# Offsetting the second recurrent stream of a two-block transformer kernel by 24 steps, with the modulation's products spread over every third step and lambda's vectors loaded at the start

## The reference, cut to what matters

```
def step(state, inp):                        # rwkv7, 8 heads of 64, 512 positions
    r_t, w_t, k_t, v_t, kk_t, b_t = inp
    sa = einsum('bhij,bhj->bhi', state, -kk_t)
    state = state * w_t[:, :, None, :] + sa[..., None] * b_t[:, :, None, :] \
          + v_t[..., None] * k_t[:, :, None, :]
    return state, einsum('bhij,bhj->bhi', state, r_t)
...
lam_full = exp(sum(lam[0] * lam[1])) - exp(sum(lam[2] * lam[3])) + lambda_init   # differential attention
bias = rel_bias[_t5_bucket(dist)]                                                # a table by distance
...
mod = (silu(c) @ ada_w[l] + ada_b[l]).reshape(B, 3, 3, 1, D)                     # second block, layer l
```

## Time and profile before

| what | value |
|---|---|
| median of three executions | 4032.23 us (4018.51 to 4037.8) |
| profiled execution, its own time | 4021.96 us |
| its span | 4020.2 us |
| mean granted TensorE clock | 0.946 of full speed |
| PE busy | 3671.3 us (91%) |
| DVE busy | 1983.7 us (49%) |
| ACT busy | 1333.8 us (33%) |
| POOL busy | 106.4 us (3%) |
| the recurrent loop | 57.5 to 492.0 us of the span |

### The profile page before, as it was taken

How to read it: one execution, slowest core, us unless ns; L and a number is a source line. 1 busy time by engine, 2 the same in 40 slices (tenths; PEclk the granted TensorE clock), 3 DMA queues, 4 the chain that set the end, 5 groups by cost and what they waited for, 6 DMA issues and landing times.

```text
span 4020.2 us, 46185 instructions
## 1 busy us (share of the span) xinstructions
PE 3671.3 (91%) x19278; PEld 2833.2 (70%) x19278; DVE 1983.7 (49%) x3434; ACT 1333.8 (33%) x2347; POOL 106.4 (3%) x204
## 2 busy tenths in 40 slices
PE   6687668699899989999899989999999889999998
PEld 4575545478688868886766768887888756677886
DVE  4767635555564655455454453334333455444333
ACT  3223213453353532232433332223222344433222
POOL 0000010000000000000000000000000000000000
PEclk9798878799999999999999999999999989999999
DMA  4232241025333325453211223332333211032332
GB/s 148 80 100 75 70 136 34 22 84 158 100 125 100 118 79 198 127 176 102 75 32 43 62 75 100 94 95 84 94 95 99 91 54 39 27 92 85 95 95 68
DMA packets 100672, 364.30 MB, mean 91 GB/s; under 512 B 11664, under 2 KB 11728, under 8 KB 99952
## 3 DMA queue, kind: packets, MB, share of 16 engines
q1 hardware_dynamic: 75888, 272.14, 21.9%
q0 software_dynamic: 24576, 89.21, 7.0%
HBM read 359.20 MB, written 2.10 MB: 90 GB/s over the span
## 4 chain that ended last, share of the span: by engine, by line
PE 87%; DVE 9%; ACT 3%; DMA 1%; issue 1%; POOL 0%; DVEq 0%; ACTq 0%; POOLq 0%
PE ps_run L369 86%; PE ps_run L613 1%; DVE rt L1548 1%; DVE nrm L1555 1%; DVE nrm L1558 1%; DVE mb L1635 1%; DVE HL L1555 1%; DVE rt L1558 1%; DMA mb<-ada 0%; ACT nrm L939 0%; ACT bias L939 0%; ACT L939 0%; ACT rt L939 0%; DVE rt L1552 0%; DVE rt L1555 0%
## 5 line engine op out<-in xcount | busy, mean ns | idle before, releaser
L369 PE MATMUL ps_run<-HH,wh 128*128 128x512 f32 x2800 | 1128.9, 403 | 91.0 <-DVE HL L1555 48.1
L369 PE MATMUL ps_run<-HL,wh 128*128 128x512 f32 x2800 | 1104.8, 395 | 0.0
L369 PE MATMUL ps_run<-HH,wl 128*128 128x512 f32 x2800 | 1103.6, 394 | 0.0
L1548 DVE TENSOR_TENSOR wl<-st,wh 128x1024 fp32r<-128x1024 f32 x511 | 625.6, 1225 | 875.6 <-ACT wh L939 874.8
L939 ACT ACTIVATE wh<-st 128x1024 fp32r<-128x1024 f32 x511 | 537.8, 1053 | 752.3 <-PE ps_run L369 751.8
L369 PEld LDWEIGHTS ps_run<-HH,wh 128*128 128x128 f32 x2800 | 533.0, 190 | 247.8 <-DVE HL L1555 70.2
L369 PEld LDWEIGHTS ps_run<-HH,wl 128*128 128x128 f32 x2800 | 534.0, 191 | 114.0
L369 PEld LDWEIGHTS ps_run<-HL,wh 128*128 128x128 f32 x2800 | 534.6, 191 | 108.2 <-issue 3.8
L369 PE MATMUL ps_run<-AH,wh 128*128 128x512 f32 x1040 | 413.2, 397 | 0.0
L369 PE MATMUL ps_run<-AL,wh 128*128 128x512 f32 x1040 | 409.9, 394 | 0.0
L369 PE MATMUL ps_run<-AH,wl 128*128 128x512 f32 x1040 | 409.8, 394 | 0.0
(11 more groups left out here) (333 smaller groups left out, 3743.9 us busy)
## 6 DMA issues: line engine op xcount, KB each, us to landing
st<-wst SPq DMA_DIRECT2D x511, 512.0 KB, 3.5
mb<-ada POOLq DMA_DIRECT2D x144, 512.0 KB, 3.9
cw<-cw POOLq DMA_DIRECT2D x4, 1024.0 KB, 6.2
X<-xT SPq DMA_DIRECT2D x8, 256.0 KB, 7.9
X<-xT POOLq DMA_DIRECT2D x8, 256.0 KB, 4.2
out<-X SPq DMA_DIRECT2D x8, 256.0 KB, 2.0
mb<-cond POOLq DMA_DIRECT2D x2, 512.0 KB, 6.9
cs<-rope POOLq DMA_DIRECT2D x2, 512.0 KB, 3.8
```

What stands on the lines that cost most here:

```text
L369: i = self.e.matmul(out, lhsT, rhs, start=start, stop=stop, skip_group_check=True)
L1548: self.e.tensor_tensor(out, a, b, op).then_inc(*self.w.done(*points))
```

## The change

Three edits. Stream 1 does nothing in its first 24 turns, and so runs 24 steps behind stream 0 on each engine. Products of the modulation are made in steps with n % 3 equal to 2. `lt` and `lam` get a place of their own, and POOL loads `lt` right after the constants. The loop is then 340 + 24 = 364 single steps long: 24 of stream 0 with an empty turn between them (n from 0 to 47), 146 pair-steps (n from 48 to 339), and 24 of stream 1 alone (n from 340 to 363).

```
+def later(steps, gen):
+    for _ in range(steps):
+        yield
+    yield from gen
...
+        self.lt, self.lam = self.sb("lt", 4), self.sb("lam", 4)
...
-        self.lt, self.lam = r("lt", 4), r("lam", 4)
...
# in Pe.program, Act.program and Dve.program
-        for n, _ in enumerate(alternate(self.rwkv(0), self.rwkv(1))):
+        for n, _ in enumerate(alternate(self.rwkv(0), later(24, self.rwkv(1)))):
             if n % 6 in (1, 3):
                 next(gb, None)
# in Dve.program
-            elif n % 6 == 5:
+            elif n % 3 == 2:
                 next(fill0, None)
# in Pool.program
         self.load(m.vec, d["vec"], "const_loads", ("consts",))
+        self.load(m.lt[0:64, :], d["lam"], "lambda_load", ("lambda",))
...
         for i in range(8):
             self.load(m.X[i], d["xT"][i], "x_again", *([("x again",)] if i == 7 else []))
-        w.wait_ge("act rwkv")
-        w.wait_ge("dve rwkv")
-        w.wait_ge("pe rwkv")
-        self.load(m.lt[0:64, :], d["lam"], "lambda_load", ("lambda",))
```

## The result

The changed kernel took 4041.34 us (median of 20 executions, 4034.18 to 4053.09), the kernel before 4023.82 us (median of 20, 4018.51 to 4037.8). The ratio is 1.0042, with a 95% interval of 1.0033 to 1.005: slower by some 17 us, where 36 us less had been forecast (3996 us, in a range of 3960 to 4036).

The account below looks back on a forecast made before the run. Neither DVE nor PE was full in the recurrent loop, both streams wanting the same engine at once, and a 39.2 us hole followed. Loop +9.5 and after it -45.6 made -36 from 4032.2: 3996 us, range 3960 to 4036.

Parts of the forecast that it names:

- After the loop: Behind the loop: fewer bias groups gain 9.5 us and a smaller hole before lambda 36.1, together 45.6 us.
- Head and tail: Loop's ends, 24 steps of one stream alone each: 63 us (bounds 51 to 69) and 37 us (23 to 45).
- The pair-steps: Loop's middle, 146 steps with both streams active: 344 us, including 66 for linears and 8 for four single ones.
- X: Loop: dense stage beside the other stream's steps 17 to 33, seven groups; four at 37.5 us, three at 30.5.
- Y: Loop: 7 pair-steps, steps 17 to 23 beside 34 to 40; 15.5 us with products, 12.5 without.
- The mates: Loop's pair-steps: all seven dense stages were taken to stand beside steps 17 to 33 of the other stream.
- The bounds: Limits for X: its busiest engine, 31 us less over the loop; no idle filled (42 and 35), 32 more.
- The sign of the clock: Loop's dense stages: a granted clock above 0.8 was listed as what would show the forecast.
- rival 1: The loop gets shorter too, mates keeping PE's clock up: -31 us there, -67 in all, 3965 us; chance 0.21.
- rival 2: Loop: eight extra table loads bring unfilled norm waits, +23 us, so -13 in all, 4019 us; chance 0.21.
- The other rule: Skill's advice for the loop: regimes bound by different engines may gain by interleaving, applied to X; no size given.
- Rival 3: Loop bound by handoffs, pair-steps at 2.56 us whatever the mates: loop +79, whole +33 us, 4065 us; chance 0.13.

Follow-up runs that it names:

- e1: The changed kernel without the 24 empty turns, both streams in lockstep, the other edits kept: 3989.43 us, ratio 0.9922 to the kernel before.
- e4: The changed kernel with 4 empty turns for 24: 4013.07 us, ratio 0.9973 to the kernel before.
- e9: The changed kernel with 44 empty turns for 24: 4019.08 us, ratio 0.9984 to the kernel before.
- e6: The changed kernel with Copy in place of the two Sqrt of each recurrence pass: 4037.9 us, ratio 1.003 to the kernel before.
- e3: The changed kernel with products at the earlier rate, n % 6 equal to 5: 4052.58 us, ratio 1.0075 to the kernel before.
- e17: The kernel before with 128 unused bytes in each partition ahead of buffer `X`, nothing else: 4008.2 us, ratio 0.9967 to the kernel before.

## Why the prediction was wrong

- **After the loop (-45.6 us forecast).** Right: -45.1. 7 groups were left, they took 6.3 us for 6.0 (573.22 to 579.55), and PE waited 2.82 us for 3.1.
- **Head and tail.** Right within their bounds: 59 us for 63, and 41.8 for 37. A doubling round alone took 4.4 us, not 3.8: PE ran its products at half clock there (the tail has 0.66), 1.97 and 1.12 us for the 2.0 in the sum.
- **The pair-steps (344 us forecast, 412.9 measured).** This is the step that failed: "of the idle I keep half". The seven groups X were to take 37.5 and 30.5 us; the first four took 44.0, 46.3, 44.1 and 40.2, the last three 41.3, 35.5 and 40.2, 50 us more in all. The two Y took 17.4 and 19.8 for 15.5 and 12.5. The linears took 72.9 for 66, the single ones 11.2 for 8. DVE's busy time was forecast to within 3 us of a group. But on balance none of the idle was filled by the mate; there was more of it. Adding up the halves of what each stage takes in lockstep and then keeping half of the idle assumes that a stage leaves to its mate the time that it doesn't use. The same pair-steps, by halves of e1's, are 380 us with nothing filled, 36 above the forecast, and 33 came on top. My reading is that in lockstep both chains wait at the same place for the same thing, and one wait serves both, while unlike stages have two waits, each with a piece of the other's chain within. The norm at 398 us shows one such wait, and e4 and e9 fit it (streams 4 steps apart lose 0.1 us a pair-step, unlike stages 0.23). Each single wait wasn't counted, and the clock has a share that is open.
- **The mates were misread.** The sum gave all seven dense stages the steps 17 to 33 as mates. By the order of the steps only the second and the sixth have these; the fourth has 20 to 36, and the other four have 24 to 40. With the prices of the earlier trace rows the mate's half is then (10/17 x 27.4 + 15.8) / 2 = 16.0 us for 13.7, some 10 us over all seven, which were missing before any question of idle time. It also fits that of the last three groups the sixth is the short one.
- **The bounds.** They had been drawn at "no idle filled", 42 and 35 us for X. Five of the seven groups lie beyond: the bound itself was too kind.
- **The sign of the clock.** "Above 0.8 in dense stages" didn't come: the seven groups have 0.65, 0.70, 0.66, 0.79, 0.71, 0.80 and 0.71. The other stream's products didn't keep the clock up, as rival 1 had it, and the doubling rounds lost their 1.00.
- **The table loads, rival 2.** The count was right (17 for 9) and the price wrong: e6 puts 15 of them at nothing to 5 us. By the 2.66 us for a switch that the Trainium skill states, in ScalarE: Activation LUTs, "What ACT_TABLE_LOAD costs", eight would have made 21 us, an estimate. The loads are 1.28 us each in the trace, as that page has them without the drain, but weren't what the chains waited for longest.
- **The other rule**, that interleaving regimes may help (the Trainium skill, Perfetto Trace Analysis, "Optimization Strategy"), had been the reason for rival 1 and for X. The runs disagree with it for this way of interleaving: e1 with the regimes together is 48 us faster than the changed kernel with them apart.
- **Rival 3 (slower)** had the loop at +79 us, the measured number, but that is luck: it kept pair-steps at lockstep's price (2.56) and had steps alone at 2.56 too. Alone they took 2.0 on average (97.1 / 48), and the pair-steps 2.83. Its sign and its point of decision (a loop above 480) held. For the whole it had +33 us; the measured 17 and the 13 us of the bytes below make 30.
- **The products.** In lockstep 16 more in the loop cost 20.1 us (e1), with the offset 12 cost 9.4 (e3), where rival 3 had 18 for 16. DVE waited for a slab only once in the loop, 0.7 us.
- **Not seen at all:** the 128 bytes, -13 us. Without them the change would have been slower by some 30. And the base of 4032.2 was the median of three executions; twenty put it at 4023.8.

## What to carry to other kernels

Two streams in lockstep on in-order engines can share waits: here one latency and one table load served both, and the doubling rounds ran at full clock. To set them apart pays only if the filled idle time exceeds the steps alone at both ends (here 24 us for an offset of 24) and the second set of waits (33 us here); don't count idle time as filled without a row that shows one stage working inside the wait of the other. Write out which step stands beside which before pricing a pair. And measure a stretch against the same steps in the other kernel, not against its mean. Test the parts of a change alone before dropping it: here two of three edits gain 31 us (13 of them by the place of tiles that one of them moves), and the third costs 48.

## What the runs showed of the hardware

- The place of tiles in SBUF changes the pace of matmuls. With `AH` at 448 bytes past a multiple of 2048 from `wh`, fp32r matmuls of 128x512 on `AH` and `AL` start every 233.4 ns (means over some 1000 starts of each kind), with 320 bytes every 226.5 to 231.8 by kind, with none every 227, as those on `HH`, which lies a multiple of 2048 bytes from `wh`. That is 13 us of this kernel for 128 bytes (e17): 1.6, 4 and 6.9 ns less at each start for 1040 matmuls of each kind. Three distances were tried, so a rule isn't shown.
- Nearly the same matmuls ran at a mean granted clock of 0.83 in lockstep (e1) and of 0.76 with the offset. Doubling rounds, at 1.00 in lockstep, now had a dense stage beside them, and the seven such groups had 0.65 to 0.80. 16 small products took 1.12 us in the tail, at half clock, for 0.68 at full clock.
- A matmul of 0.22 us that nobody waits for cost the lockstep loop 0.23 us each (73.3 us for 324), as if all of it lay on the chain, though PE was idle for 130 us of that loop. In the offset loop it cost 0.08 us (25.8 us for 327).
